# Single tiles behind the norms and another order of attention's jobs in a hybrid encoder step

## The chip, the cores and the metric

One core of a Trainium2 chip runs the whole kernel. The metric is the device time of one execution in microseconds (us); smaller is better. TensorE (PE, with its weight loads PEld), VectorE (DVE), ScalarE (ACT), GpSimd (POOL) and SyncE (SP) have a queue of instructions each and wait for each other by semaphores that are written out by hand.

## The reference, cut to what matters

Two layers, 256 prompt tokens and 8 streams of 16 tokens: T = 384 tokens, width D = 1024, all in fp32. Every sub-layer is a residual with a LayerNorm, and the next sub-layer starts from the modulated result:

```python
h = x * (1 + scale) + shift                       # per stream, from adaLN
x = layer_norm(ALPHA * x + gate * sublayer(h), g, b)
# layer 0: ffn, conv module (with a LayerNorm and silu inside), ffn
# shared k, v, log-forget projections
# layer 1: ffn, forgetting attention, ffn
```

That makes seven norms, n = 0 to 6: after ffn 0, inside the conv module (n = 1), after the conv module's output projection (n = 2), after ffn 1, after ffn 2, after attention's output projection (n = 5), and after ffn 3 (n = 6, the output).

## The kernel before, in words

All activations lie feature-major: eight tiles k of 128 features by 384 tokens (`z`, `xa`, `hH`, `hL`). A product in near-fp32 is three fast passes: activations and weights are split into a high part (`hH`, `wH`) and a rest (`hL`, `wL`), and PE does high by high, rest by high, high by rest (`unit`, L1455 to L1464; `lead`, L1466 to L1494). Weights stream from HBM through a ring of four units: SP's DMA to `raw`, ACT makes `wH` (`refill`, L763), DVE makes `wL` (L1019).

A norm works like this. PE sums over features with a matmul by `ones` (`stats`, L1540 to L1548). The sums over the tiles are gathered ahead of it on POOL (`zs` at L621 and L624, `sqs` at L630 and L633), the squares `sqb` come from ACT (L782), and PE adds only tile 7 by itself. The mean goes to `mS` on ACT (L786), the deviation through a Sqrt on ACT (L788, its table loaded at L834, L887 or L907) and a transpose on DVE to `rstd` (L1078). Then DVE's `normalise` (L1050 to L1105) walks over the tiles: `mean_out` (L1054, z minus mean), `scaled` (L1061, times rstd). Behind every scaled tile ACT computes h for the prompt's 256 columns (L807), POOL for the streams' 128 columns per tile in two operations (L660 times scale, L663 plus shift), ACT copies h to `hH` (L812), and DVE takes the rest, `hL = h - hH` (`rest`, L1152). ACT's copy of a group waits for POOL, and DVE's rest waits for ACT. The grouping is set by `PARTS` (L102): tiles 0 and 1 singly, then pairs (2,3), (4,5), (6,7). POOL leaves tile 0 to DVE (`first_streams`, L1107).

Meanwhile PE does gap blocks, small matmuls for later modulations (L1499), and then `lead`: it goes over the k tiles, at each k doing three passes for 4 weight units (3 behind n = 1, 2 behind attention), and waits for `hl_done` of tile 0, tile 1, tiles 2 and 3 together, tiles 4 and 5 together. It does tiles 6 and 7 last, behind one wait for all eight.

The depthwise conv (PE, `taps`, L1630) needs the taps of each tile, loaded by `load_taps` into two slots; the last load is issued by ACT's queue (L883) when the slot comes free. SP then issues the gap pieces in one row (L516): two and one into `gapH`, three into `gapL`.

Attention is a software pipeline over `JOBS` (L115): eight head pairs of the prompt ("p") and eight streams ("s"). In iteration n PE does scores(n), turn(n-3) (the transpose of a stream's result), values(n-2), transposes(n-1). ACT does soft(n) (exponentials), evac_t(n-1), and for n = 4 to 7 a weight refill; DVE does row_max(n), out(n-2), norm(n), the refill for n = 4 to 7, and out_stream(n-3), which a later turn waits for. SP streams K and V per stream.

Of the kernel before, what the change touches and what calls it, by code (L numbers as in the profile page):

```python
# [17 lines left out]
ALU = mybir.AluOpType  # L18
# [3 lines left out]
P = 128  # L22
# [79 lines left out]
PARTS = ((0, 1), (1, 1), (2, 2), (4, 2), (6, 2))  # L102
# [12 lines left out]
JOBS = (("p", 0), ("p", 1), ("s", 0), ("s", 1), ("p", 2), ("s", 2), ("p", 3), ("s", 3), ("p", 4), ("s", 4), ("p", 5),  # L115
# [28 lines left out]
def build_program(nc, W, ADA0, ADA, par_d, con_d, x_d, c_d, conv_d, cw_d, kt_d, v_d, lf_d, wf_d,  # L144
                  y_o, kT_o, v_o, lf_o, conv_o, nc_d):
    with ExitStack() as ctx:
# [182 lines left out]

        FIRST_STREAMS = {0: 1, 2: 2, 3: 3, 4: 5, 5: 6}  # L330
# [4 lines left out]
        FFN_LN = [0, 3, 4, 6]  # L335
        CENTERED, CENTERED_POOL = (0, 2, 6, 8, 10, 14), (0, 2, 2, 4, 6, 6)
# [21 lines left out]
        def window(ap, q):  # L358

            return (ap[:, q:q + SEQ],  # L360
                    ap[:, HIST + SEQ:UROW].rearrange("p (b t) -> p b t", b=DB)[:, :, q:q + DS])

# [39 lines left out]
        def _(sp):  # L402
# [200 lines left out]
        def _(pool):  # L603
# [13 lines left out]
            def add_tile(n, k):  # L617

                pool.wait_ge(z_ready, 2 + KT * n + k + 1)
                if k == 2:  # L620
                    g.tensor_tensor(zs[:], z[:, 1, :], z[:, 2, :], ALU.add).then_inc(ys_done, 1)  # L621
                elif k > 2:
                    pool.wait_ge(ys_done, 5 * n + k - 2)
                    g.tensor_tensor(zs[:], zs[:], z[:, k, :], ALU.add).then_inc(ys_done, 1)  # L624

            def add_square(n, k):

                pool.wait_ge(sq_done, KT * n + k + 1)
                if k == 1:
                    g.tensor_tensor(sqs[:], sqb[:, 0], sqb[:, 1], ALU.add).then_inc(sqs_done, 1)  # L630
                else:
                    pool.wait_ge(sqs_done, 6 * n + k - 1)
                    g.tensor_tensor(sqs[:], sqs[:], sqb[:, k % 2], ALU.add).then_inc(sqs_done, 1)  # L633

            def sums(n):

                for q in ((0,) if n in (2, 5) else (0, 2, 3)):
                    center(n, q)
                for k in range(1, KT - 1):
                    add_tile(n, k)  # L640
                    add_square(n, k)

            def modulate(mi):
# [5 lines left out]
                for k0, nk in PARTS:  # L649
                    ks = slice(k0, k0 + nk)  # L650
                    if k0 == 0 and FIRST_STREAMS.get(n) == mi:
                        continue
# [102 lines left out]
        def _(act):  # L755
# [18 lines left out]
            def square(n, k):  # L774

                if k == 0:
                    act.wait_ge(y0_done, n + 1)
                else:
                    act.wait_ge(z_ready, 2 + KT * n + k + 1)
                if k >= 2:  # L780
                    act.wait_ge(sqs_done, 6 * n + max(1, k - 2))
# [10 lines left out]
            def split_h(m, mi, src, dst):  # L792
# [5 lines left out]
                for k0, nk in PARTS:  # L798
# [83 lines left out]
            act.wait_ge(cv_mm, KT - 2)  # L882
            load_taps(act, KT - 1)  # L883
# [113 lines left out]
            for k in range(KT):  # L997
                c = 6 * KT + k
                act.wait_ge(zn_done, KT * 6 + max(k + 1, 2 * (k // 2) + 2 if k > 1 else 0))
# [6 lines left out]
        def _(dve):  # L1006
# [43 lines left out]
            def normalise(n, h=None, gap=(), second=bank[5]):  # L1050
# [31 lines left out]
                if n in FIRST_STREAMS:  # L1082
                    first_streams(n, FIRST_STREAMS[n])
# [18 lines left out]
                if h:  # L1102
                    rest(*h, 6, 2)
# [3 lines left out]
            def first_streams(n, mi):  # L1107

                dd = streams((kv32 if mi == 3 else h32)[:, 0:1, SEQ:T])
                dve.wait_ge(ab_done, mi)  # L1110
                dve.wait_ge(zn_done, KT * n + 1)
                v.tensor_tensor(dd, streams(z[:, 0:1, SEQ:T]), over_tokens(Am[:, mi % 2, 0:1, 1:NG], 1), ALU.mult)\
                    .then_inc(hs1_done, 1)
                dve.wait_ge(hs1_done, KT * mi + 1)
                v.tensor_tensor(dd, dd, over_tokens(Bm[:, mi % 2, 0:1, 1:NG], 1), ALU.add).then_inc(hs_done, 1)
# [333 lines left out]
        def _(pe):  # L1449
# [16 lines left out]
            def lead(n0, movH, movL, ready, before={}, units=RING, together=1):  # L1466
# [73 lines left out]
            def stats(n, gap=(), second=bank[5]):  # L1540
                pe.wait_ge(ys_done, 5 * (n + 1))
                mm(MEAN[:, 0:T], ones, zs[:], start=True, stop=False)
                pe.wait_ge(sqs_done, 6 * (n + 1))
                mm(VAR[:, 0:T], ones, sqs[:], start=True, stop=False)
                pe.wait_ge(z_ready, 2 + KT * (n + 1))
# [268 lines left out]


# [130 lines left out]
```

## Time and profile before

| what | value |
|---|---|
| median of 3 runs | 1627.47 us (1623.56 to 1629.12) |
| the profiled execution | 1623.21 us, span 1621.4 us |
| PE busy | 1568.0 us, 97% of the span |
| DVE, ACT, POOL busy | 790.1, 591.5, 249.6 us |
| DMA | 301.65 MB, mean 186 GB/s |
| granted TensorE clock | mean 0.995 |

Times in rows are us from the start of the span. In a timeline row the first number is the start, the second the duration; in brackets stands how long the engine had been idle before it, and what ended that. Matmuls overlap, so PE's bracket counts from the end of the last matmul, which is later than its issue slot.

### The profile page before, as it was taken

How to read it: one execution, taken by the hardware profiler on the slowest of the kernel's cores; microseconds unless marked ns; L12 is line 12 of the kernel's file. 1: busy time of each engine (PE TensorE's matmuls, PEld its weight loads, DVE VectorE, ACT ScalarE, POOL GpSimd, SP SyncE). 2: the span in 40 equal slices, each digit the busy share in tenths (PEclk: the TensorE clock that was granted, in tenths of full speed). 3: DMA queues.
4: the chain of work that ended last, by engine and by line, in shares of the span. 5: the costliest groups of instructions: out<-in, count | busy, mean ns of one | idle time of the engine just before them, and what ended most of it. 6: DMA issues, size and time to landing. Idle time of an engine off the chain costs nothing.

```text
span 1621.4 us, 30943 instructions
## 1 busy us (share of the span) xinstructions
PE 1568.0 (97%) x12430; PEld 1489.0 (92%) x12430; DVE 790.1 (49%) x1185; ACT 591.5 (36%) x872; POOL 249.6 (15%) x272
## 2 busy tenths in 40 slices
PE   6999999999999999999999999999999989999996
PEld 5999999988798999999888999999997789999996
DVE  3433335565487434344654434345557684444444
ACT  3433333342155333333343433333346444333332
POOL 1100002240334000012230000002252051000121
PEclk9999999999999999999999999999999999999998
DMA  9545456469972554556417555556556723333441
GB/s 367 179 158 191 171 205 240 154 227 280 293 299 87 189 178 170 191 195 226 156 53 248 184 190 172 180 196 245 191 206 239 270 92 129 122 126 120 139 143 39
DMA packets 86747, 301.65 MB, mean 186 GB/s; under 512 B 10784, under 2 KB 14160, under 8 KB 85328
## 3 DMA queue, kind: packets, MB, share of 16 engines
q1 hardware_dynamic: 83296, 294.09, 52.3%
q10 hardware_dynamic: 3360, 6.26, 1.4%
q8 instruction: 67, 1.10, 0.3%
q14 instruction: 24, 0.20, 0.0%
HBM read 283.31 MB, written 6.32 MB: 179 GB/s over the span
## 4 chain that ended last, share of the span: by engine, by line
PE 88%; DVE 5%; ACT 2%; issue 2%; DMA 2%; POOL 1%; SPq 1%; ACTq 0%; DVEq 0%; POOLq 0%
PE bank L1462 71%; PE bank L1470 6%; PE bank L1499 3%; PE bank L1690 2%; PE bank L1630 2%; DMA land<-ADA 1%; DVE z L1061 1%; DVE z L1054 1%; PE bank L1779 1%; DVE hL L1152 1%; DVE wL L1019 1%; PE bank L1748 1%; PE bank L1726 0%; DMA taps<-cw_d 0%; ACT wH L763 0%
## 5 line engine op out<-in xcount | busy, mean ns | idle before, releaser
L763 ACT ACTIVATE wH<-raw 128x1024 fp32r<-128x1024 f32 x328 | 346.0, 1058 | 506.3 <-PE bank L1462 466.5
L1462 PE MATMUL bank<-hH,wH 128*128 128x384 f32 x1496 | 504.6, 337 | 0.9 <-DVE wL L1019 0.9
L1462 PE MATMUL bank<-hH,wL 128*128 128x384 f32 x1496 | 500.3, 334 | 0.0
L1019 DVE TENSOR_TENSOR wL<-raw,wH 128x1024 fp32r<-128x1024 f32 x328 | 415.0, 1291 | 174.5 <-ACT wH L763 171.5
L1462 PE MATMUL bank<-hL,wH 128*128 128x384 f32 x1496 | 499.8, 334 | 0.0
L1462 PEld LDWEIGHTS bank<-hH,wH 128*128 128x128 f32 x1496 | 280.8, 188 | 8.1 <-issue 7.3
L1462 PEld LDWEIGHTS bank<-hL,wH 128*128 128x128 f32 x1496 | 280.9, 188 | 0.4
L1462 PEld LDWEIGHTS bank<-hH,wL 128*128 128x128 f32 x1496 | 280.8, 188 | 0.0
L1197 DVE TENSOR_TENSOR tmp<-sg,bank 128x384 f32<-128x384 f32 x88 | 48.8, 554 | 444.2 <-PE bank L1462 423.0
L1462 PE MATMUL bank<-hidH,wH 128*128 128x384 f32 x704 | 237.4, 337 | 0.0
L1462 PE MATMUL bank<-hidH,wL 128*128 128x384 f32 x704 | 235.3, 334 | 0.0
L1462 PE MATMUL bank<-hidL,wH 128*128 128x384 f32 x704 | 235.2, 334 | 0.0
L611 POOL TENSOR_TENSOR z<-z,cS 128x384 f32<-128x384 f32 x7 | 8.1, 1159 | 915.9 <-ACT cS L772 915.9
L825 ACT ACTIVATE sg<-bank 128x384 f32<-128x384 f32 x88 | 43.4, 493 | 268.0 <-PE bank L1462 244.1
L1462 PEld LDWEIGHTS bank<-hidH,wH 128*128 128x128 f32 x704 | 132.1, 188 | 2.3 <-issue 1.8
L1462 PEld LDWEIGHTS bank<-hidL,wH 128*128 128x128 f32 x704 | 132.2, 188 | 0.5
L1462 PEld LDWEIGHTS bank<-hidH,wL 128*128 128x128 f32 x704 | 132.1, 188 | 0.0
L1470 PE MATMUL bank<-hH,wH 128*128 128x384 f32 x232 | 80.9, 349 | 13.3 <-DVE hL L1152 10.6
L1470 PE MATMUL bank<-hH,wL 128*128 128x384 f32 x232 | 78.5, 338 | 0.7 <-issue 0.7
L1470 PE MATMUL bank<-hL,wH 128*128 128x384 f32 x232 | 78.3, 337 | 0.0
L633 POOL TENSOR_TENSOR sqs<-sqs,sqb 128x384 f32<-128x384 f32 x35 | 52.0, 1485 | 147.8 <-ACT sqb L782 147.8
L1470 PEld LDWEIGHTS bank<-hH,wH 128*128 128x128 f32 x232 | 44.0, 190 | 19.5 <-DVE hL L1152 14.7
(209 smaller groups left out, 1517.2 us busy)
## 6 DMA issues: line engine op xcount, KB each, us to landing
raw<-W SPq DMA_DIRECT2D x328, 512.0 KB, 3.8
araw<-ADA SPq DMA_DIRECT2D x88, 512.0 KB, 6.2
land<-ADA SPq DMA_DIRECT2D x16, 512.0 KB, 15.2
gapE<-ADA SPq DMA_DIRECT2D x16, 512.0 KB, 4.1
KTb<-kt_d SPq DMA_DIRECT2D x8, 1024.0 KB, 7.2
Vb<-v_d SPq DMA_DIRECT2D x8, 1024.0 KB, 5.2
gapH<-ADA SPq DMA_DIRECT2D x12, 512.0 KB, 6.2
gapL<-ADA SPq DMA_DIRECT2D x12, 512.0 KB, 5.0
```

What stands on the lines that cost most here:

```text
L633: g.tensor_tensor(sqs[:], sqs[:], sqb[:, k % 2], ALU.add).then_inc(sqs_done, 1)
L763: a.activation(wH[:, slot, :], raw[:, slot, :], ACT.Copy).then_inc(w_hi, 1)
L825: a.activation(sg[:, j, :], bank[2 * j][:, 0:T], ACT.Silu).then_inc(sg_done[fi], 1)
L1019: v.tensor_tensor(wL[:, slot, :], raw[:, slot, :], wH[:, slot, :].bitcast(F32), ALU.subtract)\
L1054: v.tensor_tensor(z[:, ks, :], z[:, ks, :], mS[:].unsqueeze(1).to_broadcast([P, nk, T]), ALU.subtract)\
L1061: v.tensor_tensor(z[:, ks, :], z[:, ks, :], rstd[:].unsqueeze(1).to_broadcast([P, nk, T]), ALU.mult).then_inc(zn_done, nk)
L1197: v.tensor_tensor(tmp[:, j, :], sg[:, j, :], bank[2 * j + 1][:, 0:T], ALU.mult)\
L1462: op = mm(out, tile_w(w, slot, k), m[:, k0 + k, :], start=start and k == 0 and q == 0, stop=stop and k == nk - 1 and q == 2)
L1470: op = mm(bank[j][:, 0:T], tile_w(w, j, k), m[:, k, :], start=k == 0 and q == 0, stop=k == KT - 1 and q == 2)
L1499: op = mm(out[32 * j:32 * j + 32, 0:cols], cact[:, k, :], tile[:, cols * j:cols * j + cols], start=start, stop=stop)
L1630: op = mm(acc, taps4[:, s, q, rows], src, start=q == 0, stop=q == QUADS - 1)
L1690: op = mm(bank[4 * half + t][:, :], h[:, k, tok], w[:, j, 512 * kk:512 * kk + 512], start=k == 0 and q == 0, stop=k == KT - 1 and q == 2)
```

## The change

`PARTS` becomes eight single tiles; the old grouping stays as `START_PARTS` for the first modulation alone (POOL's `modulate`, ACT's `split_h`). `lead` waits tile by tile, except for ffn 0. `normalise` walks singly: mean_out(k), rest(k-2), scaled(k). For n = 6 tiles 3 to 7 take another way: PE computes z minus mean into a bank (two fp32 matmuls by the identity), from a negated mean that ACT writes to `cS`, and DVE multiplies the bank by rstd. For n = 2 POOL adds tiles 1 to 5 and PE sums tile 6 too. In `projected` the Sqrt table is loaded before the last refill. The last `load_taps` goes from ACT's to SP's queue, between the gap pieces. `JOBS` has s1, s2 one place later: (s0, s1) no longer follow each other, (s2, s3) now do.

```diff
-PARTS = ((0, 1), (1, 1), (2, 2), (4, 2), (6, 2))
+START_PARTS = ((0, 1), (1, 1), (2, 2), (4, 2), (6, 2))
+PARTS = tuple((k, 1) for k in range(D // P))
...
-JOBS = (("p", 0), ("p", 1), ("s", 0), ("s", 1), ("p", 2), ("s", 2), ("p", 3), ("s", 3), ("p", 4), ("s", 4), ("p", 5),
+JOBS = (("p", 0), ("p", 1), ("s", 0), ("p", 2), ("s", 1), ("p", 3), ("s", 2), ("s", 3), ("p", 4), ("s", 4), ("p", 5),
         ("s", 5), ("s", 6), ("p", 6), ("s", 7), ("p", 7))
...
+        LAST_MEANS, LAST_BANKS = 3, (0, 1, 2, 3, 7)
+        SUMMED = [KT - 1 if n == 2 else KT for n in range(7)]
...
             sp.wait_ge(w_used, U_PW2)
-            for s, kq in ((0, 2), (0, 3), (1, 0), (1, 1), (1, 2), (1, 3)):
+            for s, kq in ((0, 2), (0, 3), (1, 0)):
                 piece(B_CONV_GAP[s], kq)
+            sp.wait_ge(cv_mm, KT - 2)
+            load_taps(sp, KT - 1)
+            for kq in range(1, 4):
+                piece(B_CONV_GAP[1], kq)
...
-                for k in range(1, KT - 1):
+                for k in range(1, SUMMED[n] - 1):
                     add_tile(n, k)
                     add_square(n, k)
...
-                for k0, nk in PARTS:
+                for k0, nk in PARTS if mi else START_PARTS:
...
                 a.activation(mS[:], MEAN[:, 0:T], ACT.Copy).then_inc(ms_done, 1)
+                if n == 6:
+                    a.activation(cS[:], MEAN[:, 0:T], ACT.Copy, scale=-1.0).then_inc(ms_done, 1)
...
             square(1, KT - 4)
-            act.wait_ge(cv_mm, KT - 2)
-            load_taps(act, KT - 1)
             square(1, KT - 3)
...
                     if d > 1:
                         square(n_ln, d - 1)
+                    if d == KT - 1:
+                        a.preload_act_table(ACT.Sqrt)
                     refill(u + RING + d, d % RING)
...
-                a.preload_act_table(ACT.Sqrt)
                 square(n_ln, KT - 1)
...
-                mean_out(2, 2)
-                scaled(2, 2)
-                if h:
-                    rest(*h, 1, 1)
-                mean_out(4, 2)
-                scaled(4, 2)
-                if h:
-                    rest(*h, 2, 2)
-                mean_out(6, 2)
-                if h:
-                    rest(*h, 4, 2)
-                scaled(6, 2)
-                if h:
-                    rest(*h, 6, 2)
+                    mean_out(2, 1)
+                    scaled(2, 1)
+                    mean_out(3, 1)
                     rest(*h, 1, 1)
+                    scaled(3, 1)
+                    for k in range(4, KT):
+                        mean_out(k, 1)
+                        rest(*h, k - 2, 1)
+                        scaled(k, 1)
+                    rest(*h, KT - 2, 1)
+                    rest(*h, KT - 1, 1)
+                else:
+                    mean_out(2, 1)
+                    scaled(2, 1)
+                    for k in range(LAST_MEANS, KT):
+                        dve.wait_ge(c_mm, 7 + k - LAST_MEANS + 1)
+                        v.tensor_tensor(z[:, k, :], bank[LAST_BANKS[k - LAST_MEANS]][:, 0:T], rstd[:], ALU.mult)\
+                            .then_inc(zn_done, 1)
...
-                    if k < 2:
+                    if k < 2 or ready:
                         pe.wait_ge(hl_done, KT * ready + k + 1)
...
                 mm(VAR[:, 0:T], ones, sqs[:], start=True, stop=False)
+                for k in range(SUMMED[n] - 1, KT - 1):
+                    pe.wait_ge(z_ready, 2 + KT * n + k + 1)
+                    mm(MEAN[:, 0:T], ones, z[:, k, :], start=False, stop=False)
+                    pe.wait_ge(sq_done, KT * n + k + 1)
+                    mm(VAR[:, 0:T], ones, sqb[:, k % 2], start=False, stop=False)
...
+            def last_tile(k):
+                mm(bank[LAST_BANKS[k - LAST_MEANS]][:, 0:T], ident, z[:, k, :], start=True, stop=False)
+            def last_mean(k):
+                mm(bank[LAST_BANKS[k - LAST_MEANS]][:, 0:T], ident, cS[:], start=False, stop=True).then_inc(c_mm, 1)
+            last_tile(LAST_MEANS)
+            last_tile(LAST_MEANS + 1)
+            pe.wait_ge(ms_done, 8)
+            last_mean(LAST_MEANS)
+            last_mean(LAST_MEANS + 1)
+            for k in range(LAST_MEANS + 2, KT):
+                last_tile(k)
+                last_mean(k)
```

Left out are the counters that follow from it (`sums_before(n)` in the waits on `ys_done` and `sqs_done`), a wait of ACT's first square of n = 3 on `var_ok`, ACT's wait per single tile at the end, and a parameter of `first_streams` that keeps its value.

## Rows read from the trace of the kernel before

**Rows 1.** The page, busy time by engine.
```profile
PE 1568.0 (97%) x12430; PEld 1489.0 (92%) x12430; DVE 790.1 (49%) x1185; ACT 591.5 (36%) x872; POOL 249.6 (15%) x272
```

**Rows 2.** Waits of PE: releaser, us in total, times, longest; one piece of the chain.
```profile
PE bank L1470 <- DVE hL L1152: 10.6, 9, 1.8
...
66.28 16.86 PE bank L1462 x96
```

**Rows 3.** Timeline of PE behind norm 0: lead's k = 1 and k = 2.
```profile
332.49 0.45 PE L1470 MATMUL bank<-hH,wH 128*128 128x384 f32 x1 [0.17 <-DVE hL L1152]
...
336.67 0.45 PE L1470 MATMUL bank<-hH,wH 128*128 128x384 f32 x1 [1.82 <-DVE hL L1152]
```

**Rows 4.** Timeline of POOL and DVE behind norm 0.
```profile
330.15 1.00 POOL L663 TENSOR_TENSOR h<-h,Bm 128x128 f32<-128x128 f32 x1
...
331.89 0.55 DVE L1152 TENSOR_TENSOR hL<-h,hH 128x384 fp32r<-128x384 f32 x1
...
332.36 1.38 DVE L1054 TENSOR_TENSOR z<-z,mS 128x768 f32<-128x768 f32 x1
...
335.28 1.33 DVE L1152 TENSOR_TENSOR hL<-h,hH 128x768 fp32r<-128x768 f32 x1 [0.25 <-ACT hH L812]
```

**Rows 5.** Groups by form over the span: busy us, mean ns of one, idle before.
```profile
L660 POOL TENSOR_TENSOR h<-z,Am 128x128 f32<-128x128 f32 x6 | 3.2, 527 | 45.7 <-DVE z L1061 32.3 <-DMA z<-x_d 13.4
...
L663 POOL TENSOR_TENSOR h<-h,Bm 128x128 f32<-128x128 f32 x6 | 4.8, 802 | 0.5
```

**Rows 6.** Timeline of PE and DVE behind norm 1.
```profile
450.60 1.93 PE L1499 MATMUL bank<-gapC,cact 128*32 128x128 f32 x64
...
457.21 0.44 PE L1470 MATMUL bank<-hH,wH 128*128 128x384 f32 x1 [1.04 <-DVE hL L1152]
...
462.80 0.96 DVE L1152 TENSOR_TENSOR hL<-h,hH 128x768 fp32r<-128x768 f32 x1 [2.39 <-ACT hH L896]
```

**Rows 7.** The last taps: PE's wait; the DMAs of gapH (issues, us to landing).
```profile
439.62 0.40 PE L1630 MATMUL bank<-u_own,taps 128*32 128x256 f32 x1 [3.35 <-DMA taps<-cw_d]
...
L417 SPq DMA_DIRECT2D gapH<-ADA x3: 483/606/1547, 429.5 to 430.6; - x3
...
DMA to landing us min/median/max: 6.0/7.4/9.1
```

**Rows 8.** Timeline of PE, DVE at the sums of norm 2.
```profile
490.44 0.91 PE L1542 MATMUL bank<-zs,con 128*128 128x384 f32 x2 [1.50 <-POOL zs L624]
...
493.04 0.58 DVE L1065 STREAM_TRANSPOSE mT<-bank 128x384 f32<-128x384 f32 x1 [0.57 <-PE bank L1546]
```

**Rows 9.** Timeline of ACT and DVE at the sums of norm 5.
```profile
1319.26 1.28 ACT L907 ACT_TABLE_LOAD   x1
...
1322.08 0.58 DVE L1069 STREAM_TRANSPOSE vT<-bank 128x384 f32<-128x384 f32 x1 [0.88 <-PE bank L1548]
```

**Rows 10.** Timeline of attention: PE's two waits, DVE's row maxima of jobs 5 and 8.
```profile
1236.62 0.41 PE L1789 MATMUL bank<-con,om 128*128 128x128 f32 x2 [1.59 <-DVE z L1420]
...
1249.29 0.65 PE L1779 MATMUL bank<-Vb,PT 128*32 128x128 f32 x16 [0.88 <-ACT PT L968]
...
1231.11 0.78 DVE L1383 TENSOR_REDUCE nmx<-bank 128x1 f32<-128x272 f32 x2
...
1246.59 1.01 DVE L1380 TENSOR_REDUCE nmx<-bank 128x2 f32<-128x256 f32 x2
```

**Rows 11.** Timeline of ACT and PE in the value projection.
```profile
854.59 3.15 ACT L812 ACTIVATE hH<-kv 128x384 fp32r<-128x384 f32 x5 [10.08 <-DMA nc_d<-lfA]
...
860.35 0.47 PE L1690 MATMUL bank<-wH,kvH 128*128 128x512 f32 x1
```

**Rows 12.** Timeline of DVE and ACT at the end (norm 6).
```profile
1611.02 0.56 DVE L1061 TENSOR_TENSOR z<-z,rstd 128x384 f32<-128x384 f32 x1
...
1612.55 0.96 DVE L1061 TENSOR_TENSOR z<-z,rstd 128x768 f32<-128x768 f32 x1
...
1617.40 1.30 ACT L1000 ACTIVATE z<-z,par 128x384 f32<-128x384 f32 x2 [0.63 <-DVE z L1061]
```

More of the change, by code:

```diff
@@ L328, in build_program @@
                 (3, 3, V_KV, True), (3, 3, V_L1, False), (4, 4, V_L1 + 3, False), (5, 5, V_L1 + 6, False)]
+        LAST_MEANS, LAST_BANKS = 3, (0, 1, 2, 3, 7)
+        VECTOR_STREAMS = 1
         FIRST_STREAMS = {0: 1, 2: 2, 3: 3, 4: 5, 5: 6}
@@ L361, in window, with sums_before @@
                     ap[:, HIST + SEQ:UROW].rearrange("p (b t) -> p b t", b=DB)[:, :, q:q + DS])
+        def sums_before(n):
+            return sum(SUMMED[:n]) - 3 * n
         def over_tokens(ap, k):
@@ L622, in add_tile @@
                 elif k > 2:
-                    pool.wait_ge(ys_done, 5 * n + k - 2)
+                    pool.wait_ge(ys_done, sums_before(n) + k - 2)
                     g.tensor_tensor(zs[:], zs[:], z[:, k, :], ALU.add).then_inc(ys_done, 1)
@@ L631, in add_square @@
                 else:
-                    pool.wait_ge(sqs_done, 6 * n + k - 1)
+                    pool.wait_ge(sqs_done, sums_before(n) + n + k - 1)
                     g.tensor_tensor(sqs[:], sqs[:], sqb[:, k % 2], ALU.add).then_inc(sqs_done, 1)
@@ L648, in modulate @@
                     pool.wait_ge(ab_done, mi)
-                for k0, nk in PARTS:
+                for k0, nk in PARTS if mi else START_PARTS:
                     ks = slice(k0, k0 + nk)
-                    if k0 == 0 and FIRST_STREAMS.get(n) == mi:
+                    if k0 < VECTOR_STREAMS and FIRST_STREAMS.get(n) == mi:
                         continue
@@ L779, in square @@
                     act.wait_ge(z_ready, 2 + KT * n + k + 1)
+                if k == 0 and n == 3:
+                    act.wait_ge(var_ok, n)
                 if k >= 2:
-                    act.wait_ge(sqs_done, 6 * n + max(1, k - 2))
+                    act.wait_ge(sqs_done, sums_before(n) + n + max(1, k - 2))
                 a.activation(sqb[:, k % 2], z[:, k, :], ACT.Square).then_inc(sq_done, 1)
@@ L797, in split_h @@
                     act.wait_ge(a_mm, last_in("H", FFN_GAP[mi // 2]))
-                for k0, nk in PARTS:
+                for k0, nk in PARTS if mi else START_PARTS:
                     if mi is not None:
@@ L998, in _ @@
                 c = 6 * KT + k
-                act.wait_ge(zn_done, KT * 6 + max(k + 1, 2 * (k // 2) + 2 if k > 1 else 0))
+                act.wait_ge(zn_done, KT * 6 + k + 1)
                 op = a.activation(z[:, k, :], z[:, k, :], ACT.Identity, bias=pcol("ln_b", c), scale=pcol("ln_g", c))
@@ L1082, in normalise @@
                 if n in FIRST_STREAMS:
-                    first_streams(n, FIRST_STREAMS[n])
+                    first_streams(n, FIRST_STREAMS[n], 0)
                 mean_out(1, 1)
@@ L1089, in normalise, with first_streams @@
                     rest(*h, 0, 1)
-                mean_out(2, 2)
-                scaled(2, 2)
-                if h:
+                    mean_out(2, 1)
+                    scaled(2, 1)
+                    mean_out(3, 1)
                     rest(*h, 1, 1)
-                mean_out(4, 2)
-                scaled(4, 2)
-                if h:
-                    rest(*h, 2, 2)
-                mean_out(6, 2)
-                if h:
-                    rest(*h, 4, 2)
-                scaled(6, 2)
-                if h:
-                    rest(*h, 6, 2)
+                    scaled(3, 1)
[12 more added lines that the diff above has]
+                            .then_inc(zn_done, 1)
                 for s, out in zip(gap, (ADB, second, MEAN)):
                     modulation(s, out)
-            def first_streams(n, mi):
-                dd = streams((kv32 if mi == 3 else h32)[:, 0:1, SEQ:T])
+            def first_streams(n, mi, k):
+                dd = streams((kv32 if mi == 3 else h32)[:, k:k + 1, SEQ:T])
                 dve.wait_ge(ab_done, mi)
-                dve.wait_ge(zn_done, KT * n + 1)
-                v.tensor_tensor(dd, streams(z[:, 0:1, SEQ:T]), over_tokens(Am[:, mi % 2, 0:1, 1:NG], 1), ALU.mult)\
+                dve.wait_ge(zn_done, KT * n + k + 1)
+                v.tensor_tensor(dd, streams(z[:, k:k + 1, SEQ:T]), over_tokens(Am[:, mi % 2, k:k + 1, 1:NG], 1),
+                                ALU.mult)\
                     .then_inc(hs1_done, 1)
-                dve.wait_ge(hs1_done, KT * mi + 1)
-                v.tensor_tensor(dd, dd, over_tokens(Bm[:, mi % 2, 0:1, 1:NG], 1), ALU.add).then_inc(hs_done, 1)
+                dve.wait_ge(hs1_done, KT * mi + k + 1)
+                v.tensor_tensor(dd, dd, over_tokens(Bm[:, mi % 2, k:k + 1, 1:NG], 1), ALU.add).then_inc(hs_done, 1)
             def prepare_first(pair):
```

4 lines of the change are left out of this document (2 added, 2 removed).

## The prediction, made before the change was run

> **What bounds the kernel now.** I read the page first: PE is busy 1568.0 us of a span of 1621.4 [rows 1]. The kernel is bound by TensorE, and a change that leaves its matmuls alone can win back some of 53 us at most. Next I read PE's waits. Besides the start, which this change leaves as it is, the largest group is `lead` waiting for DVE's rest of h: 10.6 us in nine waits [rows 2], plus two of the same kind on kv. They stand behind the norms, so I read the timeline of each norm, then the places of the smaller waits: the last taps, the sums of norms 2 and 5, attention, the end. The change adds fp32 matmuls to PE in two places only: two where PE waits now (norm 2), ten where PE has nothing else (the end).
>
> **1. The five norms followed by a modulated lead of 4 units (n = 0, 2, 3, 4, 5).** The five show the same pattern, so one is worked out. 96 matmuls take 16.86 us [rows 2], so the 12 of one tile take 2.1 us. Behind norm 0 PE starts k = 1 at 332.49 and could start k = 2 at 334.6; it starts at 336.67, because tiles 2 and 3 are handed over as a pair [rows 3]. So 2.1 us are lost (the bracket says 1.82, since it counts from the last matmul's end). Four more tiles at 2.1 bring PE to the last wait, for all eight tiles, at 345.1. Without a loss it would be there at 332.49 + 5 x 2.1 = 343.0. The gain is at most 2.1 us, and it asks for the rest of tile 7 by 343.0.
>
> When is that rest ready? The new order on DVE from the rest of tile 1, at 331.89 [rows 4], is rest 1, scaled 3, four times (mean, rest, scaled), rest 6, rest 7. Single operations follow each other every 0.5 us where POOL is idle (a pair at the end takes 0.96 [rows 12]; the single one ahead of it 0.56, and its successor starts sooner than it ends). Fourteen of them give 331.89 + 7.0 = 338.9. To that comes what POOL costs DVE. The trace has it for pairs: 1.38 and 1.33 us where POOL works beside [rows 4], against 0.96 alone; with the scaled operation between them that is about 1.0 per pair, 0.5 per tile. The lower bound is nothing. I take 0.35, nearer to the pairs, since POOL's elements are the same and only its operations double: five tiles, 1.75 us, so scaled 7 ends at 340.7. Behind it stand POOL's two operations, 0.53 + 0.80 [rows 5], with handovers of 0.2, ACT's copy 0.52, and DVE's rest 0.55: 342.8 to 343.2. POOL's own path gives the same: it ends tile 1 at 331.15, and six tiles at 0.53 [rows 5] + 1.00 (the slowest, beside DVE [rows 4]) + 0.2 = 1.73 end at 341.5, plus 1.3 for copy and rest: 342.8. So the last wait is nearly on time. Some slip in a loop over three engines is likely; I take 1.6 us of 2.1 per norm: **8.0 us**, bounds 0.4 x 5 = 2.0 (0.5 per tile and POOL at 2.0) and 10.5.
>
> **2. Norm 1 (3 units, no POOL).** PE's gap blocks end at 452.5 [rows 6], a tile takes 9 x 0.175 = 1.58 us, so k = 6 could start at 462.0; it started at 463.8, behind the rest at 462.80 [rows 6]. In the new order DVE needs 3 x 0.5 us per tile, ACT 1.2 (silu 0.70, copy 0.50); the last scaled ends near 460.4, then silu, copy and rest: 462.4. **1.2 us** (0.8 to 1.9).
>
> **3. The last taps.** PE waited 3.35 us [rows 7]. The load leaves ACT's queue and stands on SP's behind three pieces of gapH, ahead of gapL. The last of those three was issued at 430.6 and landed 9.1 us later, at 439.7 [rows 7]; the taps, issued at 431.8 by ACT, landed at 439.6. Both landed together, so what the taps waited for was that all four transfers were through; behind the third piece instead of beside it they land at the same time. I take **0**; bounds: 0.5 us later (SP issues after its piece, at 432.3), or 1.7 earlier if gapL shared the bandwidth before (more can't come, POOL's last sum of squares ends at 443.4). The Trainium skill has a rule on this ("DMA: Bandwidth & Descriptors", Queues, rings and completion order): every DMA engine takes turns between the rows of SP and ACT, so a lone load on ACT's row gets a share of its own, which the move gives up. By that rule the taps should have landed well before the gapH piece, and would now lose the 0.5 us of the lower bound, which makes the sum 11.6 instead of 12.1; the rows show no such lead.
>
> **4. Sums of norm 2.** PE waited 1.50 us for POOL's sum [rows 8]. Now PE adds tile 6 itself: two fp32 sums of 0.65 us in the time of that wait. DVE's transpose of the mean, at 493.04 [rows 8], then waits for ACT's last refill, which the earlier table load puts 1.3 us later, and DVE's own behind it (1.23 us instead of 2.0, as POOL has stopped): 492.55. **0.5 us** (0 to 0.8). The two matmuls cost 1.3 if POOL had been on time.
>
> **5. The table before norm 5's last refill.** It lay between refill and square at 1319.26 [rows 9]; it moves into ACT's idle time of 2.6 us. The square starts at 1319.3, and the transpose at 1322.08 [rows 9] can follow the mean's at 1321.1. **1.0 us** (0.5 to 1.2).
>
> **6. The end.** DVE had six pair operations of 0.95 from 1611.49, ACT's last pair ended at 1618.70 [rows 12]. Now tile 2 takes two single ones and tiles 3 to 7 one each: ready at 1615.1 and every 0.5 us. ACT becomes the chain: six tiles at 0.65 from 1612.65 end at 1616.6, 2.1 us earlier; the last DMA follows the one before more closely, so **1.8 us** (1.0 to 2.1). PE needs ten matmul pairs of 0.65; the mean is negated at 1608.7, so the banks are ready at 1610.1 to 1614.0, ahead of DVE. That cover needs the full clock.
>
> **7. The shared k, v stage.** ACT's copies of h for ffn 2, 3.15 us for five [rows 11], become eight at 0.48: 0.7 more, and the value weights' refill stands behind them; PE started the second half at 860.35 the moment it was there [rows 11]. **-0.4 us** (-0.7 to 0). POOL's eight single modulations there have 13 us of slack. Attention's single copies are ahead of PE's 1.04 us per tile: 0.
>
> **8. Attention.** PE's wait of 1.59 us for the stream before [rows 10] goes, since s0 and s1 no longer follow each other. But from job 5 to 8 (row maxima at 1231.11 and 1246.59 [rows 10]) one loop sets the pace: row maximum 0.45, exponentials 1.0 (s) or 1.7 (p), evacuation 0.9 to 1.0, ACT's refill 1.06, DVE's 1.23, and out_stream 0.6 where there is one. Before: s2, p3, s3 with two out_streams. After: p3, s2, s3 with two. The same sum, so row maximum 8 stays at 1246.5, and values(7), which waited 0.88 [rows 10], waits longer instead: what PE saves it loses there. **0** (-1.0 to +2.4).
>
> Sum: 8.0 + 1.2 + 0 + 0.5 + 1.0 + 1.8 - 0.4 + 0 = 12.1 us. Against the profiled execution (1623.2) that is 1611.1. The runs' median is 4.3 us above it, so I forecast 1627.5 - 12 = **1615.5 us**.
>
> **The rivals.** (A) *Slower, by contention.* Nearly all of DVE's work behind a norm shares its time with POOL's, and both now have more operations. For: DVE's pairs stretch by 0.4 each, and POOL's 128-column operation took 1.00 beside DVE [rows 4] against a mean of 0.80 [rows 5]. If a POOL operation costs DVE as much as one of twice the size did, a tile costs 1.0 instead of 0.35: tile 7 ends 5 x 0.65 later, at 346.5, after 345.1. The point from which it decides is 0.73 us per tile. Then five norms lose 1.4 each; with the other terms (+4.1) the time is 1630.4. Against: the one single tile in the trace cost DVE's pair 0.2. The Trainium skill speaks for this rival twice: GpSimd's SBUF interfaces are shared with VectorE for operations with two SBUF inputs ("GPSIMD Engine Reference", Specifications), and many small tiles pay a fixed latency each ("VectorE: DVE Perf Modes", the TRN2 errata). (B) *The last wait takes half back:* tile 7 late by 1.7 us in every norm, 2.0 instead of 8.0: 1621.4. (C) *All goes well:* 10.5 for the norms, 1.7 for the taps, 2.4 in attention: 1627.5 - 18.7 = 1608.8. (D) *The gain is spent further on* in a wait of the conv or attention stage: 1625.
>
> **How the numbers follow.** Forecast 0.50, B 0.20, C 0.15, D 0.08, A 0.07. Sums of bounds and 2 us of scatter in a median give 1607.5 to 1622.5, which leaves out A, D and the tails. A difference under 0.3% (4.9 us) can't be told from none: faster 0.82, same 0.13, slower 0.05.
>
> **What would show it.** Behind each norm no wait at k = 2 and one of at most 1 us before the last two tiles; the taps' wait as before; the wait at L1542 gone; PE's wait for the turned stream gone and one of 1.5 us or more at values(7); the end 2 us sooner. Wrong would be waits at every k (contention), or a gain in attention.

## The result: 1.1% faster, 3.7 us more than forecast in the profiled runs

| | kernel before | changed kernel |
|---|---|---|
| median of the runs | 1625.51 us (1623.51 to 1629.12, 4 runs) | 1608.15 us (1607.41 to 1608.91, 4 runs) |
| profiled execution, time and span | 1623.21, span 1621.4 | 1607.41, span 1605.6 |
| mean granted TensorE clock | 0.995 | 0.998 |

The ratio is 0.9891, with a 95% interval of 0.9869 to 0.9912: faster. The gain is 17.4 us in the medians and 15.8 in the profiled executions, against 12.1 forecast. The time lies 7.4 us under the forecast and only 0.65 us inside the range (1607.5); 2.0 of the 7.4 are the base, as the kernel before had a median of 1627.47 when the forecast was made and of 1625.51 beside the result.

The page of the changed kernel, busy time by engine, answers to [rows 1]:

```profile
PE 1573.0 (98%) x12454; PEld 1492.4 (93%) x12454; DVE 793.0 (49%) x1246; ACT 595.2 (37%) x897; POOL 261.7 (16%) x306
```

PE is busy 5 us longer than before and the span is 15.8 us shorter, so the gain is in waiting. Waits of PE in the changed kernel (releaser, us in total, times, longest), against [rows 2]:

```profile
PE bank L1655 <- DMA taps<-cw_d: 3.6, 1, 3.6
...
PE bank L1490 <- DVE hL L1172: 2.5, 3, 1.4
...
PE bank L1804 <- ACT PT L983: 2.0, 3, 0.9
```

The largest group of before, nine waits of 10.6 us, is down to three of 2.5, and those three stand ahead of a first or second tile, not of the third. The waits for POOL's sum [rows 8], for the square [rows 9] and for the turned stream [rows 10] are gone from the list.

To place the gain, I cut the span at DVE's transpose of each norm's mean. Lengths of these stretches in us; the last six columns are experiments told below.

| stretch | before | changed | gain | forecast | pairs | wait_pairs | undo_small | taps_first | taps_first_copies | before_fill |
|---|---|---|---|---|---|---|---|---|---|---|
| start to norm 0 | 324.26 | 325.13 | -0.9 | 0 | 325.09 | 323.85 | 326.36 | 323.95 | 324.65 | 324.69 |
| norm 0 to 1 | 122.28 | 122.07 | 0.2 | 1.6 | 125.50 | 123.67 | 122.75 | 118.49 | 117.97 | 123.20 |
| norm 1 to 2 | 46.50 | 44.04 | 2.5 | 1.7 | 45.95 | 44.84 | 44.60 | 45.14 | 46.22 | 46.49 |
| norm 2 to 3 | 302.49 | 298.72 | 3.8 | 1.6 | 300.93 | 300.28 | 298.76 | 298.74 | 298.75 | 300.92 |
| norm 3 to 4 | 374.89 | 372.47 | 2.4 | 1.2 | 376.43 | 374.00 | 372.49 | 372.47 | 372.45 | 374.86 |
| norm 4 to 5 | 149.99 | 147.58 | 2.4 | 1.6 | 149.23 | 148.78 | 147.73 | 148.24 | 147.73 | 149.46 |
| norm 5 to 6 | 286.80 | 283.67 | 3.1 | 2.6 | 287.41 | 285.16 | 284.60 | 283.64 | 283.62 | 286.82 |
| norm 6 to end | 14.19 | 11.92 | 2.3 | 1.8 | 11.86 | 11.92 | 14.21 | 11.83 | 11.91 | 14.26 |

Two stretches stand out: the one behind norm 0 gained almost nothing, the one behind norm 2 gained more than a lead can lose. The rest of a lead first. DVE and POOL behind norm 2 of the changed kernel, timeline (start, us, engine, line, operation, and in brackets the idle time before it with its releaser), against [rows 4]:

```profile
500.37 0.76 DVE L1172 TENSOR_TENSOR hL<-h,hH 128x384 fp32r<-128x384 f32 x1
501.05 0.76 DVE L1076 TENSOR_TENSOR z<-z,rstd 128x384 f32<-128x384 f32 x1
501.73 0.55 DVE L1069 TENSOR_TENSOR z<-z,mS 128x384 f32<-128x384 f32 x1
502.19 0.76 DVE L1172 TENSOR_TENSOR hL<-h,hH 128x384 fp32r<-128x384 f32 x1
...
509.09 0.56 DVE L1172 TENSOR_TENSOR hL<-h,hH 128x384 fp32r<-128x384 f32 x1 [0.91 <-ACT hH L828]
```
```profile
501.88 0.65 POOL L672 TENSOR_TENSOR h<-z,Am 128x128 f32<-128x128 f32 x1 [0.50 <-DVE z L1076]
502.62 0.60 POOL L675 TENSOR_TENSOR h<-h,Bm 128x128 f32<-128x128 f32 x1
503.71 0.65 POOL L672 TENSOR_TENSOR h<-z,Am 128x128 f32<-128x128 f32 x1 [0.50 <-DVE z L1076]
```

One tile takes 502.19 - 500.37 = 1.82 us. DVE's operations follow each other without a gap. Two of the three are stretched from 0.55 to 0.76; the mean keeps 0.55. POOL waits 0.50 us for DVE in each tile, so DVE sets the pace. 1.82 is less than the 2.1 us that PE needs per tile, so PE never catches up. Its lead, as one piece of the chain of waits:

```profile
499.35 14.87 PE bank L1490 x84
```

That is the tiles 1 to 7 (84 matmuls) in one go. The last rest ends at 509.65; PE asks for it at 499.35 + 5 x 2.1 = 509.85. The margin is 0.2 us. Behind norm 0 it is 0.1.

The odd stretches are a matter of the clock. Windows of the kernel before behind norm 2 (busy us of PE, PEld, DVE, ACT, POOL; then the granted clock, DMA share, GB/s), and under them the changed kernel at the last taps:

```profile
504.00:506.00 2.00, 0.54 (x3) 0.54 (x4) 1.92 (x2) 0.96 (x2) 1.75 (x2) 1.00 0.00 0
506.00:508.00 2.00, 2.00 (x8) 2.00 (x7) 1.40 (x2) 0.84 (x1) 0.00 (x0) 0.50 0.00 0
508.00:510.00 2.00, 2.00 (x9) 2.00 (x9) 1.13 (x2) 0.83 (x2) 0.63 (x1) 0.64 0.01 4
510.00:512.00 2.00, 2.00 (x13) 2.00 (x12) 0.26 (x1) 1.11 (x2) 1.95 (x4) 1.00 0.00 0
```
```profile
436.00:438.00 2.00, 0.00 (x0) 0.00 (x0) 2.00 (x6) 0.22 (x1) 2.00 (x7) 1.00 1.03 409
438.00:440.00 2.00, 1.42 (x16) 0.74 (x20) 1.27 (x2) 0.00 (x0) 2.00 (x2) 0.72 1.01 410
440.00:442.00 2.00, 2.00 (x24) 1.08 (x20) 0.00 (x0) 0.00 (x0) 2.00 (x3) 0.50 1.04 416
442.00:444.00 2.00, 2.00 (x52) 1.40 (x48) 0.00 (x0) 0.00 (x0) 0.04 (x1) 0.93 1.02 408
```

After the wait of 1.8 us that the change removes, the kernel before ran some 3.5 us at the lower of the two levels (0.50, 1.2 GHz). The changed kernel has no wait there, but has such a spell behind its wait for the last taps, which cost nothing of the kind in the profiled execution of before. The pieces of the chain give the price: the 112 matmuls of the last taps took 4.76 us before and take 6.45 us now.

```profile
430.49 8.05 DMA taps<-cw_d
438.54 0.04 issue
438.58 6.45 PE bank L1655 x112
```

So the hypothesis for the experiments: the single tiles carry most of the gain, 2.1 us a norm; each long wait of PE can cost 1.7 us more in clock, gained once (norm 2) and lost once (taps); the small parts are worth what was forecast and the order of attention nothing. Rivals: the gain is from the small parts or the order; the clock spells have another cause.

### The profile page after: what moved, and what is told of

The parts are those of the page before. It is cut to its first block, busy times and chain, and to the rows that moved or that the text cites. A ratio compares the mean times of both kernels' runs of the same rounds, so it can differ in the third digit from the quotient of the medians.

```text
span 1605.6 us, 31043 instructions
## 1 busy us (share of the span) xinstructions
PE 1573.0 (98%) x12454; PEld 1492.4 (93%) x12454; DVE 793.0 (49%) x1246; ACT 595.2 (37%) x897; POOL 261.7 (16%) x306
## 4 chain that ended last, share of the span: by engine, by line
PE 90%; DVE 5%; DMA 2%; ACT 1%; issue 1%; SPq 1%; ACTq 0%; DVEq 0%
PE bank L1482 71%; PE bank L1490 8%; PE bank L1519 4%; PE bank L1655 2%; DVE wL L1034 1%; DMA land<-ADA 1%; PE bank L1715 1%; PE bank L1804 1%; ACT wH L775 1%; PE bank L1773 1%; PE bank L1751 1%; DVE hL L1172 1%; DMA taps<-cw_d 1%; DVE z L1069 0%; DVE z L1076 0%
## 5 line engine op out<-in xcount | busy, mean ns | idle before, releaser
L1482 PEld LDWEIGHTS bank<-hH,wH 128*128 128x128 f32 x1496 | 280.8, 188 | 8.3 <-issue 7.6
L796 ACT ACTIVATE sqb<-z 128x384 f32<-128x384 f32 x56 | 28.5, 514 | 68.1 <-DVE z L1206 27.0
```

The lines of the kernel that those rows point to most:

```text
L1482: op = mm(out, tile_w(w, slot, k), m[:, k0 + k, :], start=start and k == 0 and q == 0, stop=stop and k == nk - 1 and q == 2)
```

## The experiments

Each was timed in five rounds beside the kernel before. The medians of before in the three groups of runs were 1626.38, 1627.06 and 1625.06.

**pairs: two-tile steps back behind the norms.**

```diff
-PARTS = tuple((k, 1) for k in range(D // P))
+PARTS = START_PARTS
 # normalise: mean_out(2, 2), scaled(2, 2), rest(1, 1), mean_out(4, 2), ... as before
-                    if k < 2 or ready:
+                    if k < 2:
```

> The changed kernel with two-tile steps put back behind every norm that has a lead behind it (vector engine, ScalarE, GpSimd and TensorE's waits); the order of attention, tile 6 of norm 2's sums, the Sqrt table, the last taps' queue and the end stay as changed. Theory (single tiles carry the gain: about 2.1 us per norm for six norms, and 1.7 us of half clock behind norm 2's wait): about 1622 us (1620 to 1624), a wait of about 1.8 to 2.1 us ahead of tiles 2 and 3 comes back behind each norm, and half clock behind it after norm 2. Rival (sums, table, order and end carry a good part): under 1616 us.

Measured: 1622.68 us (1621.16 to 1624.75), ratio 0.9981 (0.9972 to 0.9990). The theory holds: nearly all of the gain is gone. The 3.7 us by which this kernel still beats the kernel before are what the three small parts of undo_small are worth (3.8). Waits of PE:

```profile
PE bank L1489 <- DVE hL L1171: 10.6, 10, 1.8
...
PE bank L1654 <- DMA taps<-cw_d: 4.3, 1, 4.3
```

The cleanest price is in the stretch from norm 2 to 3, where this run shows the full clock throughout: 300.93 - 298.72 = 2.2 us for one lead. Behind norm 1 it is 1.9. The expectation failed in one point: the spell of half clock was not behind norm 2 this time but behind norm 3 and norm 5, after waits of the same 1.8 us, and behind the taps:

```profile
810.00:812.00 2.00, 1.89 (x9) 1.89 (x10) 1.75 (x3) 0.85 (x1) 0.54 (x1) 0.81 0.00 0
812.00:814.00 2.00, 2.00 (x8) 2.00 (x7) 1.43 (x2) 0.54 (x2) 0.43 (x1) 0.50 0.00 0
```

Which waits of that length are followed by a spell differs from execution to execution.

**wait_pairs: single tiles on the other engines, but PE waits for two at a time.**

```diff
-                    if k < 2 or ready:
+                    if k < 2:
```

> The changed kernel, single tiles on the vector engine, ScalarE and GpSimd as changed, but TensorE behind a norm waits for tiles 2 and 3, and 4 and 5, together again. Theory (both halves count: the finer wait, and the shorter period of the vector engine's steps): tile 3 comes 1.83 us behind tile 2, so that TensorE waits some 1.5 us ahead of tile 2 behind each norm but the first of them with three weights, and not again after; 1615 to 1619 us with some half clock behind these waits, so between the changed kernel and the one with pairs everywhere (1622.7 us). Rival 1 (the pace of the vector engine alone carries the gain): 1608 to 1610 us. Rival 2 (the finer wait alone): 1621 us or more.

Measured: 1614.94 us (1613.00 to 1616.83). Both halves count. Waits of PE:

```profile
PE bank L1490 <- DVE hL L1172: 8.1, 7, 1.4
```

Each stretch with a lead of four weights grew by 1.2 to 1.6 us, the one behind norm 1 by 0.8. How much each half is worth shows in the leads themselves. The table has the start of the last of a lead's 96 matmuls, in us behind the transpose of the norm's mean:

| lead behind norm | 0 | 2 | 3 | 4 | 5 |
|---|---|---|---|---|---|
| before | 24.86 | 26.42 | 25.06 | 24.84 | 25.82 |
| pairs | 24.84 | 24.85 | 26.66 | 24.84 | 26.43 |
| wait_pairs | 24.19 | 24.21 | 24.20 | 24.20 | 24.18 |
| changed | 22.73 | 22.65 | 22.62 | 22.92 | 22.67 |

Three of these leads hold a spell of half clock (norm 2 before, norms 3 and 5 in pairs), and norm 5's of before holds the wait for the table. In the others PE's finer wait is worth 1.3 to 1.6 us a lead, and the shorter steps of the other engines 0.6. In the medians some 7 us lie between the changed kernel and this one, and 8 between this one and pairs. Of these 8 the leads and norm 1 explain 5 x 0.64 + 1.1 = 4.3. The rest fits the clock: its mean was 0.9975 in this kernel's six executions and 0.9954 in the twelve of pairs, an estimated 0.0021 x 1622 = 3.4 us. None of these waits, 1.0 to 1.4 us long, was followed by half clock; the only spell ahead of the end was at the taps.

**undo_small: three small parts taken back, each in its own stretch.**

```diff
-        SUMMED = [KT - 1 if n == 2 else KT for n in range(7)]
+        SUMMED = [KT for n in range(7)]
 # the table for norm 5 behind the last refill; norm 6 in pairs on DVE, no matmuls
```

> The changed kernel with three of its small parts taken back, each in another stretch: GpSimd adds tile 6 of norm 2's sums again, the Sqrt table is loaded behind the last refill again ahead of norm 5, and the last norm is multiplied in pairs on the vector engine without TensorE. Theory (my terms as they stand, in the trace): the stretch from norm 1's to norm 2's transpose 0.5 to 1.5 us longer with GpSimd's wait back, the one up to norm 5 about 1.0 us longer with the wait for the square back, the end 2.3 us longer (14.2 us from norm 6's transpose); in all 1612 us (1611 to 1613.5). Rival (single tiles made these parts needless, or they hid behind each other): under 1610.5 us.

Measured: 1612.15 us (1611.03 to 1613.69), as the theory had it. PE at the sums of norm 2 and of norm 5 in this run:

```profile
491.11 0.91 PE L1559 MATMUL bank<-zs,con 128*128 128x384 f32 x2 [1.49 <-POOL zs L636]
```
```profile
1313.41 0.91 PE L1570 MATMUL bank<-sqb,con 128*128 128x384 f32 x2 [0.97 <-ACT sqb L796]
```

By stretches: sums of norm 2 worth 44.60 - 44.04 = 0.56 us, though a wait of 1.49 comes back, since PE's own two sums of 0.65 fall away; the table 284.60 - 283.67 = 0.93; the end 14.21 - 11.92 = 2.29.

**jobs_old: the old order of attention.** One line, `JOBS` as before.

> The changed kernel with attention's old order of jobs (double streams third and fourth). Theory (the order is worth nothing, two waits only change places): 1608 us within 1 us, and attention from its first score to the lead behind it as long within 0.5 us, with the waits of the kernel before back. Rival (the order is worth about 1 us, part of what the sum left out): 1609 to 1610 us.

Measured: 1607.15 us (1605.64 to 1610.45), with 0.9891 (0.9875 to 0.9907) the same ratio as the changed kernel. PE's waits in attention are of 2.9 us instead of 2.0:

```profile
PE bank L1814 <- DVE z L1440: 1.6, 1, 1.6
PE bank L1804 <- ACT PT L983: 1.3, 2, 0.9
```

The stretch from norm 4 to 5 was 148.41 us against 147.58; but the stretch varied by as much with the new order (taps_fill 148.68, undo_small 147.73), by what the profile calls "issue" (time in which nothing that it shows was awaited). One interval is free of that: from the row maximum of job 5 to that of job 8 it is 15.47 or 15.48 us in the three profiles with the old order and 15.08 to 15.10 in the ten with the new one. So the new order is worth some 0.4 us in the traces, and nothing that the times can tell.

**before_fill: the kernel before with its wait behind norm 2 filled.** Nine matmuls that nothing reads, into a free bank, ahead of the wait at k = 2.

```diff
+            def keep_busy():
+                for _ in range(9):
+                    mm(bank[4][:, 0:T], tile_w(wH, 0, 0), hH[:, 0, :], start=True, stop=True)
-                    lead(u, hH, hL, m)
+                    lead(u, hH, hL, m, {2: keep_busy} if fi == 1 else {})
```

> The kernel before with nine matmuls that nothing reads, some 1.6 us, ahead of TensorE's wait for tiles 2 and 3 behind norm 2. Theory (norm 2's wait costs its 1.8 us and 1.7 us more through the half clock behind it, so that the change gains 3.5 us there): the clock stays full from 505 to 510 us, the 72 matmuls behind the wait take 12.7 us instead of 14.3 us, and the time is 1.7 us under that of the kernel before (1.0 to 2.2). Rival (the half clock is not due to the wait): no difference, or up to 0.3 us slower.

Measured: 1627.33 us (1622.45 to 1629.08), ratio 1.0008 (0.9999 to 1.0017). In the profile the clock stays full there, and the 72 matmuls behind the wait take 12.76 us instead of the 14.33 of the kernel before (the kernel before, then this one):

```profile
505.46 14.33 PE bank L1470 x72
```
```profile
506.81 12.76 PE bank L1470 x72
```

The stretch is shorter by the same 1.57 us (302.49 to 300.92). That is the price of one spell. It does not show that the filler prevented the spell: pairs has the same wait behind norm 2, no filler, and the full clock too, with a stretch of 300.93. As a claim on the time of the kernel the expectation fell: the spell behind norm 2 belonged to that one execution, and this one had a spell behind a wait of 2.14 us for the taps of tile 6 instead (112 matmuls in 6.45 us), where the profile of before had none:

```profile
434.25 6.45 PE L1637 MATMUL bank<-u,taps 128*32 128x256 f32 x112 [2.14 <-DMA taps<-cw_d]
```

Filling one of many long waits gains nothing that the median shows, and the mean granted clock is no higher: 0.992 in this kernel's twelve executions, 0.993 in the 43 of the kernel before that were timed beside the experiments.

**taps_fill: the changed kernel with its wait for the last taps filled.** Seven matmuls on constants ahead of `taps(KT - 1)`.

> The changed kernel with seven matmuls on constants, some 3.2 us of work that nothing reads, in TensorE's queue ahead of the wait for the last taps. Theory (the idle stretch of 3.6 us is what drops the clock to its half level for about 3.5 us behind it, which costs 1.7 us): the last taps run at full clock, 4.8 us instead of 6.45 us, and the time is 1606.5 us (1605.5 to 1607.5). Rival (the half clock comes from something else, as the DMA or a rhythm of its own): the half clock stays and the time is 1608 us or more.

Measured: 1607.87 us (1605.64 to 1609.41). The clock was full throughout the stretch, and the last taps took 4.76 us:

```profile
430.30 10.01 DMA taps<-cw_d
440.31 0.04 issue
440.36 4.76 PE bank L1655 x112
```

But this time the taps needed 10.01 us to land instead of 8.05, which ate the 1.7 us. That PE's idle time brings on the spell is supported, not proven: this is one filled profile, with the DMA as busy as ever (share 1.01 to 1.05), against the unfilled ones counted under after_again. The mean granted clock of all executions points the same way: 0.9988 in the five of this kernel and 0.9979 in nine of the changed kernel, where one spell of some 3.5 us at half clock is 0.0011. What it is worth in the total is not shown.

**after_again: the changed kernel once more.** To see which of this is chance.

> The changed kernel once more, on the chip of the two kernels beside it. Theory (about every run has the half clock behind the last taps' wait of some 3.5 us, and stalls of TensorE's sequencer come on top that differ from run to run): 1608 us within 1 us, runs spread over about 4 us, the wait and the half clock behind it there again. Rival (the spell was a chance of the one profiled run): no half clock ahead of the end.

Measured: 1607.23 us (1604.50 to 1609.67). The wait was 3.9 us, the taps took 7.32 us at the lower level, and their landing 9.2 us. Over all profiles with the wait unfilled and longer than 3 us, the spell came behind it in seven of eight (the changed kernel twice, pairs, wait_pairs, undo_small, taps_act, jobs_old; not in the kernel before).

**taps_act: the last taps issued by ACT again.**

```diff
             square(1, KT - 4)
+            act.wait_ge(cv_mm, KT - 2)
+            load_taps(act, KT - 1)
             square(1, KT - 3)
```

> The changed kernel with the last taps issued by ScalarE again, behind norm 1's fifth square, and SyncE's pieces in their old order. Theory (the move of the taps is worth nothing either way, the landing goes by the bytes that are in the queues): within 1 us of the changed kernel, taps issued 1 to 2 us later than by SyncE and landing at the same time within 1 us, a wait of 3.3 to 4.3 us. Rival 1 (SyncE's queue holds them up, as they stand behind three pieces): 1 to 2 us faster. Rival 2 (the earlier issue gains its 1 to 2 us): 1 to 2 us slower than the changed kernel.

Measured: 1608.88 us (1607.60 to 1609.34), within the scatter of the changed kernel. I had expected a later issue; it came at 430.27 against 430.49, as ACT is free there. Landing took 7.5 us by ACT's queue (7.8 in the kernel before, 8.7 in before_fill) and 8.1 to 10.0 by SP's behind the pieces, in seven profiles; PE, where nothing filled its wait, waited 3.1 us here and 3.4 in the kernel before by ACT's queue, and 3.4 to 4.3 by SP's.

**taps_first: the taps ahead of the three gap pieces in SP's queue.**

```diff
-            for s, kq in ((0, 2), (0, 3), (1, 0)):
-                piece(B_CONV_GAP[s], kq)
             sp.wait_ge(cv_mm, KT - 2)
             load_taps(sp, KT - 1)
+            for s, kq in ((0, 2), (0, 3), (1, 0)):
+                piece(B_CONV_GAP[s], kq)
```

> The changed kernel with SyncE issuing the last taps ahead of the three gap pieces that now stand before them in its queue. Theory (the taps land late because 1.5 MB of pieces is in the queues before them): landing in 4 to 5.5 us instead of 8, TensorE waits under 1 us instead of 3.6 us, no half clock there, and the norm's sums become the next thing late: 1604.5 us (1603 to 1606.5). Rival (the DMA engines are full there whatever the order, and what is put behind is late instead, pieces or weights): 1607 us or more with a new wait behind norm 1.

Measured: 1607.29 us (1604.41 to 1609.44). The mechanism is shown, the size in the total is not. Landing (transfer, KB, us), here and in the changed kernel:

```profile
taps<-cw_d SPq DMA_DIRECT2D x1, 448.0 KB, 4.0
```
```profile
taps<-cw_d SPq DMA_DIRECT2D x1, 448.0 KB, 8.1
```

The wait and the spell are gone, and the stretch from norm 0 to 1 is 3.6 us shorter. The next things late were POOL's sum, as expected, and one stall of PE's sequencer in the gap blocks:

```profile
439.98 0.88 PE L1562 MATMUL bank<-zs,con 128*128 128x384 f32 x2 [1.52 <-POOL zs L636]
...
447.01 1.14 PE L1519 MATMUL bank<-gapL,cact 128*32 128x128 f32 x33 [1.21 <-issue]
```

**taps_first_fill: the same, and three matmuls ahead of the wait.**

> As the kernel with the last taps first, with three matmuls that nothing reads (1.3 us) ahead of TensorE's wait for them. Theory (that wait is then too short to lower the clock, so the filler buys nothing): within 1 us of that kernel, up to 0.8 us slower. Rival (the clock drops after short waits too): 1 to 1.7 us faster than it.

Measured: 1604.90 us (1603.42 to 1612.87), no spell at the taps with or without the filler. The medians of the two lie 2.4 us apart with ranges that overlap, which tells nothing of the filler.

**taps_first_copies: and POOL's copies of the state behind its sums.**

```diff
-                if k == 4:
+                if k == KT - 2:
```

> The changed kernel with the last taps ahead of the three gap pieces in SyncE's queue, and GpSimd's sixteen copies of the convolution's state (5 us) moved from between the sums of tiles 4 and 5 to behind those of tile 6. Theory (with the taps early, those copies are what is late: the sum of tile 6 came 1.5 us too late): no wait for the sums of norm 1, transpose of norm 1 about 5.5 us sooner after norm 0's than in the changed kernel (116.5 us), no half clock there; 1603 us (1601.5 to 1605). Rival (the copies' write to memory, started 5 us later, or the weights behind it are late instead): 1605 us or more, with a wait for weights or pieces behind norm 1.

Measured: 1604.90 us (1604.26 to 1605.14, 4 runs), ratio to before 0.9874 (0.9854 to 0.9893). POOL's sum is in time. The stretch from norm 0 to 1 is 4.1 us shorter than in the changed kernel, not 5.5, and 2.2 us are given back behind it:

```profile
448.25 1.14 PE L1519 MATMUL bank<-gapL,cact 128*32 128x128 f32 x33 [2.27 <-issue]
```

This stall lies where the DMA engines are full (share 0.99 to 1.06 from 444 to 450 us), and taps_first had one of 1.21 at the same place. The changed kernel had none, with the DMA engines as full there (1.03 to 1.04). What it waits for stays open. All four runs lie below the median of the changed kernel in the same group (1607.23), but the two intervals overlap: a likely gain of 2 us, not a settled one.

## Why the prediction was right, and where its sizes were off

The direction, the place and the mechanism were right. Term by term, in us:

| term | taken | measured | from |
|---|---|---|---|
| 1, five norms | 8.0 | 10.9 | table of the leads, less the clock behind norm 2 and the table for norm 5 |
| 2, norm 1 | 1.2 | 1.9 | pairs, norm 1 to 2 |
| 3, last taps | 0 | -0.3 | wait 3.61 for 3.35 |
| 4, sums of norm 2 | 0.5 | 0.6 | undo_small |
| 5, table | 1.0 | 0.9 | undo_small |
| 6, end | 1.8 | 2.3 | undo_small |
| 7, shared k, v | -0.4 | 0.0 | 2.4 in the stretch less 2.4 for its lead |
| 8, attention | 0 | 0.5 | 2.4 in the stretch less 1.9 for its lead |
| clock behind norm 2 | - | 1.6 | before_fill |
| clock behind the taps | - | -1.7 | 6.45 for 4.76 |
| start | - | -0.9 | table of stretches |
| sum | 12.1 | 15.8 | |

**Term 1** was the mis-sized one. Its working stood up: contention of 0.35 per tile was taken and is 0.32 (1.82 against 1.5), and the last rest was to be ready 10.3 to 10.7 us behind k = 1 (its items add up to 10.8) and was ready after 10.3. What failed is the step behind it, "some slip in a loop over three engines is likely": the 0.5 us taken off each norm. There was no slip. POOL's own path, given as an equal bound with 1.73 per tile, was wrong: with single tiles its operations take 0.65 and 0.60, 1.3 with the handover, and it idles 0.5 per tile. The 1.00 us of [rows 4] was the price beside a DVE pair, not beside a single; pairs has it again behind each of its norms. The gain per lead was 1.9 to 2.4 us, 2.2 on average, so that the sum passed even the upper bound of 10.5.

**Term 2**: the gain was the upper bound of its range; no wait of PE is left behind norm 1.

**Term 3** was right in the wait and left out what follows it. The rule weighed there, of the Trainium skill ("DMA: Bandwidth & Descriptors", Queues, rings and completion order), had the taps lose 0.5 us by leaving ACT's row. The rows lean its way: 0.3 us more of wait in the two profiles, and landing in 7.5 to 8.7 us by ACT against 8.1 to 10.0 by SP, two ranges that overlap. My reading of the rows, that all four transfers had to be through in any case, fell with taps_first: issued ahead of the pieces, the taps land in 4.0 us while the same bytes move.

**Term 6**: ACT did become the chain, starting 5.47 us behind the transpose as worked out (5.44). Its six tiles took 3.70 us, not 3.9:

```profile
1599.15 3.70 ACT L1015 ACTIVATE z<-z,par 128x384 f32<-128x384 f32 x6 [0.35 <-DVE z L1076]
```

**Term 7**: ACT's copies for ffn 2, five in 3.15 us before [rows 11], became eight in 3.43, 0.3 more and not 0.7; PE waited 0.2 us behind it.

```profile
846.60 3.43 ACT L828 ACTIVATE hH<-kv 128x384 fp32r<-128x384 f32 x8 [10.10 <-DMA nc_d<-lfA]
```

**Term 8**: the argument of the loop held nearly. The row maximum of job 8 stood at 1246.59 [rows 10], 76.17 us behind norm 4's transpose; it is at 1236.48, 74.05 behind it. Of these 2.1 us the lead gives 1.9. But the two sums that the prediction called the same differ by 0.4 us, as jobs_old shows. "One of 1.5 us or more at values(7)" was wrong: of the removed wait of 1.59 only half came back, as a new one of 0.75, and the old one of 0.88 stayed.

```profile
1233.51 0.64 PE L1804 MATMUL bank<-Vb,PT 128*32 128x128 f32 x16 [0.75 <-ACT PT L983]
1239.18 0.64 PE L1804 MATMUL bank<-Vb,PT 128*32 128x128 f32 x16 [0.86 <-ACT PT L983]
```

**The clock** was in none of the terms. In the profiled pair it gave 1.6 us and took 1.7, so it hardly changed the sum; it moved the gain from the stretch behind norm 0 to the one behind norm 2. The medians saw more of it. The profiled execution of before had a mean granted clock of 0.995; the 43 that were timed beside the experiments average 0.993, an estimated 0.002 x 1624 = 3 us more lost than in the profile. The changed kernel's nine average 0.998, as its profile does. This fits a gain that is larger in the medians (17.4) than in the profiled pair (15.8). That fewer long waits bring fewer spells would explain it, and no run counts the spells of the unprofiled executions.

**The range** was narrower than its working. The bounds of the terms add up to gains of 2.1 to 20.6 us, which is 1606.9 to 1625.4 before any scatter, and not 1607.5 to 1622.5. That the time fell inside the stated range was a near thing.

**The rivals.** A (contention) has its effect, 0.32 us per tile, and is far from its point of decision, 0.73. The Trainium skill's statement for it, that GpSimd and VectorE share SBUF interfaces ("GPSIMD Engine Reference", Specifications), fits the 0.76 us of a DVE operation beside POOL against 0.55 alone, and names no size. B would need a wait ahead of the last two tiles; there is none above 0.1 us. C came closest (1608.8 against 1608.15), but for another reason: its 10.5 in the norms are there, its 1.7 at the taps are not, and of its 2.4 in attention there are 0.5. D is what happened to norm 0's lead alone.

## What to carry to other kernels

Where one engine feeds another tile by tile, make the step as small as the handovers allow on both sides: where no clock spell came between, the finer wait gave about 1.5 us and the finer production 0.6 of the 2.1 us of a lead here. The finer wait alone was not run; tiles handed over in pairs come together, so it should find nothing to take. Compare the producer's period with the consumer's, 1.82 against 2.1 us, and the last arrival with the last need, 10.3 against 10.5; if the rows say that it just fits, take nothing off for untidiness. Look at what the granted clock does behind each long wait (here those of 1.8 us and more) before you price it, and at who stands ahead of a late transfer in its own queue before you move it to another.

## What the runs showed of the hardware that I had not expected

- POOL beside DVE is slower beside long DVE operations: 1.00 us for a 128-column operation in the kernel before [rows 4], 0.60 for the same one between single-tile operations.
- A wait of PE of 1.8 us behind a norm was followed by some 3.5 us at the lower clock in three of eleven cases (one of four in before, two of four in pairs, none of three in before_fill), one of 3.1 to 4.3 us for the taps in seven of eight, and none of 1.0 to 1.4 us ahead of a tile was. A wait of 2.1 us for the taps of tile 6 was, in before_fill. Length is not all: in attention, where PE has many small gaps, a stall of 1.04 us was followed by a spell once (taps_first_fill, clock 0.50 from 1248 to 1251 us). Each spell costs about 1.6 to 2.9 us (112 matmuls of taps in 6.45 to 7.67 us instead of 4.76).
- The same 448 KB landed in 3.7 to 5.0 us ahead of three pieces of 512 KB in its queue (three profiles), and in 8.1 to 10.0 us behind them (seven).
- PE's sequencer stalls for 0.6 to 2.3 us at places that differ between executions of kernels that are alike there. Their cause was not looked for. With the clock spells they bear on the 7 us over which 43 executions of the kernel before scatter: the 25 with a mean granted clock of 0.993 or less have a median of 1627.7 us, the other 18 one of 1624.9.
